# Seven block products in place of eight for 20 of the 22 gate/up pairs of a dense feed-forward

## The reference

```
def swiglu(h, w_gate, w_up, w_down):
    return (jax.nn.silu(h @ w_gate) * (h @ w_up)) @ w_down

h = rmsnorm(x, norm_ffn[0])                  # x: (512, 1024)
x = x + swiglu(h, ffn_w_gate[0], ffn_w_up[0], ffn_w_down[0])   # D_FF = 2816 = 22 * 128
```

## Time and profile before

| what | value |
|---|---|
| time, median of 3 runs | 1558.84 us (1557.78 to 1558.86) |
| the profiled execution | 1558.77 us, its span 1557.0 us |
| busy in the span | PE 1539.7, DVE 1008.7, ACT 832.4, POOL 236.4 us |
| gate and up stage | from about 341 to 581 us of the span |
| down stage | from 581 to about 701 us |

### The profile page before, as it was taken

How to read it: one execution, slowest core, us unless ns; L and a number is a source line. 1 busy time by engine, 2 the same in 40 slices (tenths; PEclk the granted TensorE clock), 3 DMA queues, 4 the chain that set the end, 5 groups by cost and what they waited for, 6 DMA issues and landing times.

```text
span 1557.0 us, 23251 instructions
## 1 busy us (share of the span) xinstructions
PE 1539.7 (99%) x7960; PEld 1310.2 (84%) x7961; DVE 1008.7 (65%) x1689; ACT 832.4 (53%) x1306; POOL 236.4 (15%) x290
## 2 busy tenths in 40 slices
PE   9999999999999999999999999999999999999997
PEld 6888888888888888888888888879898888889895
DVE  7657765755444443336557765776676998887587
ACT  6436665433233323224447664465576888886564
POOL 0204564000000000002015662010000011110000
PEclk9999999999999999999999999999999999999999
DMA  7832212244444333336322213518778999997783
GB/s 227 196 100 69 73 55 82 95 136 138 158 139 134 95 91 98 99 94 160 101 85 70 71 55 95 189 67 318 253 251 259 357 385 375 386 381 264 236 260 128
DMA packets 89787, 265.71 MB, mean 171 GB/s; under 512 B 12497, under 2 KB 22737, under 8 KB 89680
## 3 DMA queue, kind: packets, MB, share of 16 engines
q1 hardware_dynamic: 82864, 248.59, 47.4%
q0 software_dynamic: 6816, 15.74, 3.8%
HBM read 242.84 MB, written 19.83 MB: 169 GB/s over the span
## 4 chain that ended last, share of the span: by engine, by line
PE 97%; DVE 1%; DMA 1%; ACT 0%; issue 0%; SPq 0%; DVEq 0%; POOLq 0%; ACTq 0%
PE ps L1692 19%; PE ps L1693 19%; PE ps L1697 19%; PE ps L2046 8%; PE ps L2021 5%; PE ps L2023 5%; PE ps L2022 5%; PE ps L2048 3%; PE ps L1859 2%; PE ps L1892 1%; PE ps L2020 1%; PE ps L2019 1%; PE ps L1872 1%; PE ps L1891 1%; PE ps L1871 1%; PE ps L2007 1%
## 5 line engine op out<-in xcount | busy, mean ns | idle before, releaser
L803 ACT ACTIVATE w_hi<-raw 128x1024 fp32r<-128x1024 f32 (+1 forms) x168 | 176.0, 1048 | 337.1 <-PE ps L1697 333.9
L1692 PE MATMUL ps<-h_hi,w_hi 128*128 128x512 f32 x880 | 350.6, 398 | 0.6 <-DVE k_lo L1239 0.4
L1693 PE MATMUL ps<-h_lo,w_hi 128*128 128x512 f32 x880 | 343.6, 390 | 0.0
L1697 PE MATMUL ps<-h_hi,w_lo 128*128 128x512 f32 x880 | 343.4, 390 | 0.0
L1151 DVE TENSOR_TENSOR w_lo<-raw,w_hi 128x1024 fp32r<-128x1024 f32 x136 | 164.2, 1207 | 123.9 <-ACT w_hi L803 123.7
L1156 DVE TENSOR_TENSOR m_lo<-m_raw,m_hi 128x1024 fp32r<-128x1024 f32 x144 | 167.8, 1191 | 62.5 <-ACT m_hi L846 49.3
L1697 PEld LDWEIGHTS ps<-h_hi,w_lo 128*128 128x128 f32 x880 | 165.2, 188 | 35.7
L1692 PEld LDWEIGHTS ps<-h_hi,w_hi 128*128 128x128 f32 x880 | 165.6, 188 | 27.0 <-DVE k_lo L1239 0.8
L1693 PEld LDWEIGHTS ps<-h_lo,w_hi 128*128 128x128 f32 x880 | 166.0, 189 | 25.7 <-issue 0.7
L846 ACT ACTIVATE m_hi<-m_raw 128x1024 fp32r<-128x1024 f32 x144 | 145.3, 1030 | 55.5 <-PE ps L2020 25.3
L2046 PE MATMUL ps<-xt,m_hi 128*128 128x320 f32 x592 | 155.2, 347 | 0.3 <-issue 0.3
(11 more groups left out here) (307 smaller groups left out, 3156.3 us busy)
## 6 DMA issues: line engine op xcount, KB each, us to landing
m_raw<-moe_g SPq DMA_DIRECT2D x88, 512.0 KB, 5.2
raw<-w_in SPq DMA_DIRECT2D x68, 512.0 KB, 3.4
m_raw<-moe_down SPq DMA_DIRECT2D x56, 512.0 KB, 5.9
raw<-w_gu SPq DMA_DIRECT2D x44, 512.0 KB, 3.5
h_rows<-moe_g SPq DMA_DIRECT2D x32, 512.0 KB
h_rows<-moe_g SPq DMA_DIRECT2D x32, 384.0 KB
h_rows<-moe_down SPq DMA_DIRECT2D x24, 512.0 KB
m_raw<-moe_g SPq DMA_DIRECT2D x24, 384.0 KB, 5.5
```

What stands on the lines that cost most here:

```text
L803: A.activation(split_of(n, 0, cols)[0], raw[:, n % RAW, 0:cols], ACT.Copy).then_inc(hi_ready, 1)
L1692: E.matmul(ps[:, bank, :], wh, hi, start=first, stop=False)
L1693: E.matmul(ps[:, bank, :], wh, lo, start=False, stop=False)
L1697: return E.matmul(ps[:, bank, :], wl, hi, start=False, stop=final)
```

## The change

Pairs 0 and 1 are computed as before. For pairs 2 to 21 the product of h (2 halves of the tokens x 2 halves of the contraction) with the pair's weights (2 halves of the contraction x gate or up) is made with seven block products in place of eight, each of 128 output features x 256 tokens x 512 contraction: 4 tiles x 3 matmuls of 256 columns. Four of the seven take a sum of weight blocks and four a sum of token blocks as operand; the results are sums of the seven.

Once, during units 0 to 3: ACT makes x times gain in fp32 (8 tiles of `full`); DVE makes two token-block differences of 128x1024, POOL the other two (`t_full`); ACT splits them into highs, DVE into lows. Per pair: POOL makes four weight-block sums (128x512) in three tiles `sums`, from the raw units; ACT makes seven highs of 128x512 (`seven_high`, four products ahead) and keeps product 0's result in SBUF; DVE makes six of the lows (`seven_low`), POOL that of product 5; DVE makes the output sums in four steps (after products 1, 3, 5, 6), reading PSUM and the partial sums in SBUF. The gate is multiplied by `rms_inv` in place; the up side is not any more, and DVE scales the output of down instead, in PSUM, before it adds it to `xs`. `a_lo` of pairs 2 to 21 goes to POOL. A raw unit is free for SP's next load when all seven lows of its pair are made.

PE's instructions for a pair are 84 matmuls of 256 columns instead of 48 of 512. Further waits of PE: product 4 on product 0's copy, products 5 and 6 on the sums before them (they write into the PSUM banks that these read).

The diff, cut (the layout of the new tiles, indices of blocks and some helpers are left out):

```diff
...
+PLAIN = 2
+N_SEVEN = 7 * (KF - PLAIN)
+SEVEN0, SEVEN_END = FFN_START + 2 * PLAIN, FFN_START + N_GU
...
-a_hi = sb("a_hi", [P, KF, T], F32R, ffn)
-a_lo = sb("a_lo", [P, KF, T], F32R, ffn)
-silu = sb("silu", [P, 2, T], F32, ffn)
-act = sb("act", [P, 2, T], F32, ffn)
+a_both = sb("a_both", [P, KF, 2, T], F32R, ffn)
+a_hi, a_lo = a_both[:, :, 0, :], a_both[:, :, 1, :]
+t_low = sb("t_low", [P, 9, 2, HALF_T], F32R, ffn)
 ffn.close()
+sums = (norm, y_other, y_sum)
...
+def seven_weights(i):
+    f, q, j = seven_of(i)
+    gate, up = FFN_START + 2 * f, FFN_START + 2 * f + 1
+    low, high = slice(0, T), slice(T, UNIT)
+    return ((gate, low), (None, 1), (None, 2), (None, 0), (gate, high), (up, high), (None, 2))[j]
+def seven_full(i):
+    n, part = seven_weights(i)
+    return sums[part][:] if n is None else raw[:, n % RAW, part]
+SUM_STEP = (0, 2, 3, 1, 0, 0, 4)
+def seven_split(i):
+    b, c0 = i % 4 // 2, i % 2 * T
+    return w_hi[:, b, c0:c0 + T], w_lo[:, b, c0:c0 + T]
...
+SEVEN_AT = (0, 2, 6, 4, 1, 3, 7)
...
+def seven_low_seen(i):
+    return 6 * (i // 7) + (1, 2, 3, 4, 5, 5, 6)[i % 7]
...
+def u3_at(f):
+    return 4 * f + 6 if f + 1 < KF else 4 * f + 3
...
-        if n >= RAW:
+        if SEVEN0 <= n - RAW < SEVEN_END:
+            sp.wait_ge(seven_lo, 6 * ((n - RAW - SEVEN0) // 2 + 1))
+            sp.wait_ge(seven_lo_pool, (n - RAW - SEVEN0) // 2 + 1)
+        elif n >= RAW:
             sp.wait_ge(lo_ready, n - RAW + 1)
...
+    def weight_sums(q, part):
+        n = SEVEN0 + 2 * q
+        gate, up = raw[:, n % RAW, :], raw[:, (n + 1) % RAW, :]
+        if part == 0:
+            pool.wait_ge(raw_full[n % RAW], 16 * (n // RAW + 1))
+            pool.wait_ge(raw_full[(n + 1) % RAW], 16 * ((n + 1) // RAW + 1))
+            if q:
+                pool.wait_ge(seven_lo, 6 * (q - 1) + 4)
+            pool.tensor_tensor(sums[0][:], up[:, 0:T], up[:, T:UNIT], ALU.add).then_inc(sums_ready, 1)
+            pool.wait_ge(sums_ready, 4 * q + 1)
+            pool.tensor_tensor(sums[1][:], sums[0][:], gate[:, 0:T], ALU.subtract).then_inc(sums_ready, 1)
+        if part == 1:
+            if q:
+                pool.wait_ge(seven_lo, 6 * q)
+            pool.tensor_tensor(sums[2][:], gate[:, 0:T], up[:, 0:T], ALU.subtract).then_inc(sums_ready, 1)
+        if part == 2:
+            pool.wait_ge(sums_ready, 4 * q + 2)
+            pool.wait_ge(seven_lo, 6 * q + 3)
+            pool.tensor_tensor(sums[2][:], gate[:, T:UNIT], sums[1][:], ALU.subtract).then_inc(sums_ready, 1)
+    def low_on_pool(q):
+        i = 7 * q + 5
+        pool.wait_ge(seven_hi, i + 1)
+        hi, lo = seven_split(i)
+        pool.tensor_tensor(lo, seven_full(i), hi.bitcast(F32), ALU.subtract).then_inc(seven_lo_pool, 1)
+    def act_lo_on_pool(f):
+        pool.wait_ge(a_hi_ready, f + 1)
+        pool.tensor_tensor(a_lo[:, f, :], act_of(f), a_hi[:, f, :].bitcast(F32), ALU.subtract).then_inc(a_lo_ready, 1)
...
+        if layer == 0:
+            pool.wait_ge(h32_ready, KD)
+            pool.wait_ge(t_full_ready, 2)
+            pool.tensor_tensor(t_full(2), h_block(0, second_half), h_block(0, first_half), ALU.subtract).then_inc(t_full_ready, 1)
+            pool.tensor_tensor(t_full(3), h_block(1, first_half), t_full(0), ALU.subtract).then_inc(t_full_ready, 1)
+            for part in range(3):
+                weight_sums(0, part)
+            for q in range(1, KF - PLAIN + 1):
+                if q < KF - PLAIN:
+                    weight_sums(q, 0)
+                low_on_pool(q - 1)
+                if q < KF - PLAIN:
+                    weight_sums(q, 1)
+                if q > 1:
+                    act_lo_on_pool(PLAIN + q - 2)
+                if q < KF - PLAIN:
+                    weight_sums(q, 2)
+            act_lo_on_pool(KF - 1)
...
+            def token_parts_hi(ts):
+                for t in ts:
+                    A.wait_ge(t_full_ready, (2, 1, 3, 4)[t])
+                    for k2 in range(2):
+                        A.activation(t_split(t, k2)[0], t_pair(t, k2), ACT.Copy).then_inc(t_hi_ready, 1)
...
+            def silu(f):
+                A.wait_ge(ffn_scaled, f + 1)
+                A.activation(silu_of(f), silu_of(f), ACT.Silu).then_inc(silu_ready, 1)
+            def act_hi(f):
+                A.wait_ge(act_ready, f + 1)
+                A.activation(a_hi[:, f, :], act_of(f), ACT.Copy).then_inc(a_hi_ready, 1)
+            def seven_high(i):
+                n, part = seven_weights(i)
+                if n is None:
+                    A.wait_ge(sums_ready, 4 * (i // 7) + SUM_STEP[i % 7])
+                else:
+                    A.wait_ge(raw_full[n % RAW], 16 * (n // RAW + 1))
+                A.activation(seven_split(i)[0], seven_full(i), ACT.Copy).then_inc(seven_hi, 1)
+            for k in range(KD):
+                A.activation(h_full(k), xs[:, k, :], ACT.Copy, scale=gains[:, gain_of(1), k:k + 1]).then_inc(h32_ready, 1)
+            for u in range(2 * PLAIN):
+                n, f = FFN_START + u, u // 2
                 A.wait_ge(unit_done, n + 1)
+                if u == 1:
+                    split_hi(n + 2)
+                if u >= 2:
+                    seven_high(2 * u - 4)
+                    seven_high(2 * u - 3)
+                if u % 2 == 0:
+                    silu(f)
+                else:
+                    act_hi(f)
                 if u:
-                    split_hi(n + 2)
-                f = u // 2
-                if u % 2 == 0:
-                    A.wait_ge(ffn_scaled, f + 1)
-                    A.activation(silu[:, f % 2, :], silu[:, f % 2, :], ACT.Silu).then_inc(silu_ready, 1)
-                else:
-                    A.wait_ge(act_ready, f + 1)
-                    A.activation(a_hi[:, f, :], act[:, f % 2, :], ACT.Copy).then_inc(a_hi_ready, 1)
...
+            for i in range(N_SEVEN):
+                f, q, j = seven_of(i)
+                A.wait_ge(seven_done, i + 1)
+                if j == 0:
+                    A.activation(quarters[:, 4 * f, :], seven_bank(i), ACT.Copy).then_inc(p1_kept, 1)
+                if i + 4 < N_SEVEN:
+                    seven_high(i + 4)
+                elif i % 2:
+                    n = SEVEN_END + (i + 4 - N_SEVEN) // 2
+                    A.wait_ge(raw_full[n % RAW], 16 * (n // RAW + 1))
+                    A.activation(w_hi[:, n % SPL, :], raw[:, n % RAW, :], ACT.Copy).then_inc(hi_ready, 1)
+                if j == 0 and q:
+                    silu(f - 1)
+                if j == 3 and q:
+                    act_hi(f - 1)
+                if j == 5:
+                    A.sem_inc(hi_ready, 2)
+            silu(KF - 1)
             warm_root()
+            act_hi(KF - 1)
...
-                f = u // 2
+            def token_parts_lo(ts):
+                for t in ts:
+                    for k2 in range(2):
+                        V.wait_ge(t_hi_ready, 2 * t + k2 + 1)
+                        hi, lo = t_split(t, k2)
+                        lo_of(lo, t_pair(t, k2), hi).then_inc(t_lo_ready, 1)
...
+            def gated_up(f, up):
+                V.wait_ge(silu_ready, f + 1)
+                V.tensor_tensor(act_of(f), silu_of(f), up, ALU.mult).then_inc(act_ready, 1)
+            def seven_low(i):
+                V.wait_ge(seven_hi, i + 1)
+                hi, lo = seven_split(i)
+                lo_of(lo, seven_full(i), hi).then_inc(seven_lo, 1)
+            for u in range(2 * PLAIN):
+                n, f = FFN_START + u, u // 2
                 V.wait_ge(unit_done, n + 1)
                 if u % 2 == 0:
-                    scaled(silu[:, f % 2, :], UNIT_BANKS[u % 4]).then_inc(ffn_scaled, 1)
-                else:
-                    if f >= 2:
-                        V.wait_ge(a_lo_ready, f - 1)
-                    scaled(act[:, f % 2, :], UNIT_BANKS[u % 4]).then_inc(up_scaled, 1)
+                    scaled(silu_of(f), UNIT_BANKS[u]).then_inc(ffn_scaled, 1)
+                if u == 0:
+                    V.wait_ge(h32_ready, KD)
+                    V.tensor_tensor(t_full(1), h_block(1, second_half), h_block(0, second_half), ALU.subtract).then_inc(t_full_ready, 1)
+                    V.wait_ge(t_full_ready, 1)
+                    V.tensor_tensor(t_full(0), t_full(1), h_block(0, first_half), ALU.add).then_inc(t_full_ready, 1)
+                if u == 1:
+                    split_lo(n + 2)
+                if u >= 2:
+                    seven_low(2 * u - 4)
+                    seven_low(2 * u - 3)
+                if u % 2:
+                    gated_up(f, ps[:, UNIT_BANKS[u], :])
+                    act_lo(f)
                 if u:
-                    split_lo(n + 2)
-                if u % 2 == 1:
-                    V.wait_ge(silu_ready, f + 1)
-                    V.wait_ge(up_scaled, f + 1)
-                    V.tensor_tensor(act[:, f % 2, :], silu[:, f % 2, :], act[:, f % 2, :], ALU.mult).then_inc(act_ready, 1)
-                    V.wait_ge(a_hi_ready, f + 1)
```

(74 more changed lines are left out.)

56 lines of the change are left out of this document (50 added, 6 removed).

## The result

The changed kernel takes 1595.47 us (median of 4 runs, 1593.57 to 1597.31) against 1558.31 for the kernel before in the same comparison: ratio 1.0241, 95% interval 1.0229 to 1.0253, slower. Forecast: 1604. The profiled execution took 1594.97 us, with a span of 1593.0, 36.0 more than before.

A forecast was written before the change was run, and what follows sets the result against it. TensorE's matmul pace bounds the kernel now; after the change, DVE and POOL excluding each other on SBUF reads would. From 1558.77 us, +9 + 18 x 2.0 - 0.5 + 0.65 = +45 gives 1604 us; range 1555 to 1636 (0.80).

The forecast's parts named there:

- PE's pace: Gate and up stage: 84 matmuls of 256 columns at 0.120 us, 10.08 us a pair, 0.80 less than now.
- Contention as the bound: Gate and up pairs: POOL operations reading SBUF and DVE operations with two SBUF inputs exclude each other, 12.5 us shared.
- B: Rival, gate and up stage: no contention for operations with two SBUF inputs; -12.3 us, 1546 us; chance 0.14.
- R: Rival added with the experiments: POOL's chain of operations and waits is too long for a pair without contention; no chance given.
- S: Rival added with the experiments: DVE's own list of operations and waits is too long for a pair; no chance given.
- C: Rival, gate and up pairs: DVE and POOL take turns read by read; 10.9 us a pair, 1565 us; chance 0.08.
- D: Rival, gate and up stage: no contention, but 256-column matmuls take 0.130 us each; 1562 us; chance 0.03.
- A: The forecast, gate and up stage: DVE two-SBUF-input operations and POOL's SBUF reads shut each other out; 1604 us; chance 0.74.
- Its size: Steady gate and up pair: 7.74 us POOL, 4.80 DVE and 0.4 gaps, 12.9 us, +2.0 per pair; bounds 11.0 to 14.2.
- The pairs: Gate and up: first pair +9 us from helper work and contention, then 18 pairs at +2.0 us each.
- The end: Last pair about 10.3 us, -0.5; in down, scaling the last output on DVE costs +0.65 us.
- What would show it: Trace signs: POOL 7 to 8 us busy per pair, pairs 12 to 14 us, first near 20, clock 1.00.

The follow-up runs named there:

- e1: Changed kernel with POOL's per-pair weight sums and low cut to one column, a_lo a write of zeros; 3316.14 us whole (routing altered), steady pairs 10.03 to 10.04 us.
- e3: Changed kernel with DVE's six weight lows per pair replaced by comparisons taking one input from PSUM; 1553.46 us, ratio 0.9971 to the kernel before.
- e9: e8 with the gate product moved into DVE's gap and more late a_lo made earlier; 1546.96 us, ratio 0.993 to the kernel before.
- e2: Changed kernel with each of POOL's six operations per pair replaced by three writes of zeros, reading nothing; 3312.62 us whole, values altered.
- e5: Kernel before, plus one POOL subtraction of 128x512 with SBUF inputs per unit, started together with DVE's split; 1557.92 us, ratio 0.9998.
- e10: Kernel before, plus the extra POOL subtraction of e5 per unit at half width, 128x256; 1557.89 us in one run.
- e8: e4 with a_lo of 20 pairs moved to the last pair and down, and token sums and splits made earlier; 1550.28 us, ratio 0.995 to the kernel before.
- e4: Changed kernel with all of POOL's work in this stage moved to DVE, everything computed; 1557.55 us, ratio 1.000 to the kernel before.

## Why the prediction was right, and where it was off

**PE's pace: right.** Forecast 0.120 per matmul and 10.08 us a pair; measured 0.12 and, wherever PE is left alone, 10.03 (e1, e3, e9). The 0.130 of the earlier trace rows is not the price of a weight load every 256 columns. It is still the smaller matmul that keeps the saving down: seven eighths of 10.88 would be 9.5 us.

**Contention as the bound: right, and shown.** The step went from an attention row in which a scaling of 0.28 us ended only after POOL to operations with two SBUF inputs. e1 (next to no POOL reading), e2 (POOL writing), e3 (one DVE input out of PSUM) and e5 with e10 (turns of whole instructions) each bear out one part of it. B is refuted by e3, in the forms R and S too, C by e5 and e10, D by e1. The row at 1122.12 that counted for B speaks as little against A: DVE had started first there, and in e5 the one that is first keeps its time.

**Its size: the term that was off.** 12.9 us per steady pair; measured 12.30. The sum took 6 x 1.29 + 8 x 0.60 and 0.4 for gaps. What passes one after the other is the reading alone: 0.55 of a DVE operation and 1.11 of POOL's, the estimate that stood as lower bound (0.53 and 1.13). And two of DVE's eight (L1652 and one low) start while POOL is idle: 6 x 1.11 + 6 x 0.55 = 10.0. The rest, 2.3, goes with POOL's idle time, 2.6 a pair in place of 0.4, where it waits for lows. The two errors partly made up for each other: with the reading times right and its 0.4 kept, the sum would have had 10.4, under the measured pair by 1.9.

**The pairs: mostly right.** The forecast gave 18 pairs the contended pace; the second pair, at 10.09, had it not. Its +9 for the first pair was counted to the end of that pair, 383.4 against 374.3. Measured so, it is +12.0 (386.21 against 374.17): 9.5 in the pair and 2.6 before it, of which 0.9 came before the change. The stretch of a `w_lo` to 3.16 us before the first product (1.4 us of PE) wasn't foreseen. The forecast also held "clock still 1.00, since gaps stay under a microsecond or two", and that failed: the waits were 4.18 and 2.61 us, and matmuls ran at half clock behind both. That contention makes this pair long was right, and e1 shows it: with POOL's weight operations cut to one column it is 12.46 us (e1), near the 13.1 that the forecast had without any contention. e3's unchanged 20.30 shows that it isn't the lows from product 4 on.

**The end: right** in the scaling of the last output (+0.65: 0.62 and its issue). The last pair was put at 10.3 and took 10.9.

**The sum.** Term by term: the first pair 3.0 too little, the second 2.8 and the other 17 together 9.6 too much, the last pair and down 0.9 too little. That is 8.5 of the 9 us between 1604 and 1594.97. That the total came so near is in part luck, since errors of both signs stand in it. (The bounds of the sum give 1570 to 1628; the 1571 to 1630 under the chances is a slip of no weight.)

**What would show it.** POOL 7 to 8 us busy per pair was wrong, 9.7: the wait for the lock counts as busy time. The clock was wrong too, and two pairs (the second and the last) lay under the 12 to 14 us. The others were right: the first pair near 20 us, 17 pairs at 12.3, PSUM-input operations at 0.69, two-SBUF-input ones far above it, and PE's idle time ended by DVE's `w_lo` and POOL's low, 16.6 and 18.0 us. Of the 16.6, 6.8 are the two waits of the first pair; in the steady pairs POOL's low holds PE longer, 1.1 us against 0.6.

## What to carry to other kernels

Before work goes to an idle POOL, count DVE's operations with both inputs in SBUF and POOL's that read SBUF: where they overlap, their reading times added up here as if they ran on one engine, and POOL's operation weighed twice DVE's. With the same six operations on POOL a pair took 12.30 us, with all of them on the already busier DVE 10.55. When a saving on TensorE is small per step, compare the helpers' row of starts with it to the tenth of a microsecond: one wait of 0.16 us a pair (e8) took a fifth of the 0.86 us that the seven products can give.

## What was not expected of the hardware

- In contention an operation's busy time grows by the wait: DVE's 0.68 became up to 1.81, POOL's 1.29 up to 1.75. A page on which both engines look well used (DVE 100%, POOL 78% of the steady stretch) can be one in which each waits for the other in turn.
- POOL's turn is not one number: 1.11 to 1.15 us in after, 0.90 in e5 where both inputs are the same tile; 0.43 for 256 columns more. Which of the two differences makes it (the tile or the turn before) wasn't tried.
- After waits of 4.18 and 2.61 us in a stage otherwise full of matmuls TensorE ran at 1.2 GHz for about 3 us, and so it did after the wait of 2.2 us in e4's first pair; after waits of at most 0.72 us (e8) it didn't.
- DVE's and ACT's operations with no second SBUF input kept their 0.68 and 0.62 us through all of it.
